# The turned keys of a chunked recurrence made by VectorE in 32x32 blocks, in four buffers, with the row norm in two halves

## What is computed

```python
def step(S, inp):                      # chunks of tokens
    L = jnp.cumsum(gc, axis=1)
    o_inter = jnp.einsum('bchk,bhkv->bchv', qc * jnp.exp(L), S)
    ...
    S_new = jnp.exp(Lc)[..., None] * S + jnp.einsum(
        'bjhk,bjhv->bhkv', kc * jnp.exp(Lc[:, None] - L), vc)
    return S_new, o_inter + o_intra
...
yb = rms_norm(o, o_norm_g).astype(x.dtype).reshape(B, T, WIDTH_B) * jax.nn.silu(zb)
```

## Time and profile before

| | before |
|---|---|
| median of 3 runs | 1557.94 us (1557.22 to 1558.79) |
| span of the profiled execution | 1555.9 us |
| PE busy | 1527.1 us, 98% |
| VectorE busy | 787.0 us, 51% |
| GpSimd busy | 826.0 us, 53% |
| ScalarE busy | 540.7 us, 35% |
| mean granted TensorE clock | 0.996 of full speed |

### The profile page before, as it was taken

One profiled execution on the slowest core, in us unless ns is written; L12 is line 12 of the kernel. 1 busy time (PEld: TensorE's weight loads), 2 busy tenths in 40 slices (PEclk: granted clock), 3 DMA queues, 4 the chain that ended last, 5 costly groups with the idle time before them and its releaser, 6 DMA issues.

```text
span 1555.9 us, 31655 instructions
## 1 busy us (share of the span) xinstructions
PE 1527.1 (98%) x13048; PEld 1243.0 (80%) x13048; DVE 787.0 (51%) x1900; ACT 540.7 (35%) x1119; POOL 826.0 (53%) x1074
## 2 busy tenths in 40 slices
PE   5999999999999999999999999999999999999998
PEld 2777788877888788888779878888888978888886
DVE  4767464234558866232544774622453775623132
ACT  4334324334322532434331452243432353143330
POOL 0525434557863643365773472437786363437671
PEclk9999999999999999999999999999999999999999
DMA  9612211334453321233343231223544231222351
GB/s 339 243 55 83 83 57 55 111 133 158 168 197 108 110 70 57 82 109 108 137 164 135 92 120 43 83 66 114 208 154 149 75 110 56 78 72 91 102 167 60
DMA packets 62790, 178.94 MB, mean 115 GB/s; under 512 B 7086, under 2 KB 18695, under 8 KB 61864
## 3 DMA queue, kind: packets, MB, share of 16 engines
q1 hardware_dynamic: 62648, 176.93, 33.4%
HBM read 162.84 MB, written 11.96 MB: 112 GB/s over the span
## 4 chain that ended last, share of the span: by engine, by line
PE 95%; DVE 3%; DMA 1%; SPq 1%; issue 1%; ACT 0%; DVEq 0%
PE ps_D L758 56%; PE ps_D L755 25%; PE ps_XCD L820 2%; PE ps_XB L896 1%; PE ps_XB L949 1%; PE ps_XA L954 1%; PE ps_XA L921 1%; PE ps_XA L932 1%; PE ps_XB L948 1%; PE ps_XA L896 1%; DMA th_t<-in_w_ada 1%; SPq L507 1%; PE ps_XB L932 0%; PE ps_XCD L831 0%; PE ps_XCD L939 0%
## 5 line engine op out<-in xcount | busy, mean ns | idle before, releaser
L1702 POOL TENSOR_TENSOR w_lo_t<-w_raw,w_hi_t 128x256 fp32r<-128x256 f32 x920 | 681.0, 775 | 599.7 <-ACT w_hi_t L980 599.4
L758 PE MATMUL ps_D<-h_hi_t,w_hi_t 128*128 128x512 f32 x1024 | 411.2, 402 | 0.0
L758 PE MATMUL ps_D<-h_hi_t,w_lo_t 128*128 128x512 f32 x1024 | 399.6, 390 | 0.0
L758 PE MATMUL ps_D<-h_lo_t,w_hi_t 128*128 128x512 f32 x1024 | 399.5, 390 | 0.0
L980 ACT ACTIVATE w_hi_t<-w_raw 128x1024 fp32r<-128x1024 f32 x232 | 240.0, 1051 | 124.6 <-PE ps_D L755 61.6
L758 PEld LDWEIGHTS ps_D<-h_hi_t,w_hi_t 128*128 128x128 f32 x1024 | 192.3, 188 | 46.3 <-issue 8.9
L758 PEld LDWEIGHTS ps_D<-h_hi_t,w_lo_t 128*128 128x128 f32 x1024 | 192.2, 188 | 41.8
L758 PEld LDWEIGHTS ps_D<-h_lo_t,w_hi_t 128*128 128x128 f32 x1024 | 192.6, 188 | 36.5
L755 PE MATMUL ps_D<-w_hi_t,h_hi_t 128*128 128x384 f32 (+1 forms) x384 | 141.6, 369 | 1.0 <-DVE yf_t L1342 1.0
L755 PE MATMUL ps_D<-w_lo_t,h_hi_t 128*128 128x384 f32 (+1 forms) x384 | 136.6, 356 | 0.0
L755 PE MATMUL ps_D<-w_hi_t,h_lo_t 128*128 128x384 f32 (+1 forms) x384 | 136.3, 355 | 0.0
(11 more groups left out here) (386 smaller groups left out, 2332.9 us busy)
## 6 DMA issues: line engine op xcount, KB each, us to landing
w_raw<-in_w_blocks SPq DMA_DIRECT2D x232, 512.0 KB, 3.4
xr<-in_x_prompt SPq DMA_DIRECT2D x16, 512.0 KB, 5.0
x_or_AT<-in_x_prompt SPq DMA_DIRECT2D x14, 512.0 KB, 4.8
out_dram<-xr SPq DMA_DIRECT2D x12, 512.0 KB, 2.8
x_or_AT<-in_x_turned SPq DMA_DIRECT2D x3, 1024.0 KB, 5.6
p_or_hf<-in_x_turned SPq DMA_DIRECT2D x3, 1024.0 KB, 6.2
out_dram<-xr SPq DMA_DIRECT2D x8, 256.0 KB, 2.0
ibtok<-vtok SPq DMA_DIRECT2D x8, 192.0 KB, 3.5
```

The source lines that it names most:

```text
L758: ins = mm(bank[:, :], w[:, s0, k0 + k, :], a[:, k, :], start=go, stop=end)
L1702: ins = g_.tensor_tensor(w_lo[:, c, k:k + 2], w_raw[:, n % NRAW, k:k + 2], f32(w_hi[:, c, k:k + 2]), ALU.subtract)
```

## The change

`KT` is VectorE's alone. `turn` transposes 16 blocks of 32 partitions by 4 heads by 32 columns from `kk` straight into `kst[:, t]`, then waits for them, and a memset of one column signals `kst`. PE's four transposes, ScalarE's copy and the use of XC are gone. `kst` has four buffers, one for each chunk, in memory that the silu of za (`silu_za`) has in the attention part and the residual rows later; what else used the old buffer is now `yst`. The KT tasks stand at halves 54, 55, 56 and 58, `o` stays at 57, 59, 61 and 63, `st` too but for chunk 0, which goes from 57 to 58. PE's `st` and ScalarE's part of `o` now wait for `kst`. `onorm` is two tasks of two chunks each, at halves 60 and 64.

```diff
--- before.py
+++ after.py
@@ -89,6 +89,7 @@
                                 ("q", 2): 3}.items()}
 OUT_AT = (56.5, 57.5, 58, 59.5, 60.5, 61, 61.5, 62.5)
 S_AT, PV_AT = (18, 20, 22, 25, 27, 30, 32, 35), (24, 29, 34, 38)
+KT_AT, ON_AT = (54, 55, 56, 58), (60, 64)
 TILED = S_AT + PV_AT + tuple(range(42, 56, 2))
 SPOT, HOLDER, ATTACH, BURST_AT, PAIR = [], [], {}, {}, {}
 COST = {"A": 3, "B": 3, "pa": 2, "pb": 2}
@@ -194,10 +195,11 @@
     for _l in range(7):
         at_half(it, 42 + 2 * _l, "level", _l, "XA" if _l % 2 else "XB")
     for _t in range(NT):
-        put(it, 28 + _t, 0, "KT", _t, "XC")
-        put(it, 28 + _t, 1, "o", _t, "XB")
-        put(it, 28 + _t, 1, "st", _t, "XA")
-    put(it, 32, 0, "onorm", 0)
+        at_half(it, KT_AT[_t], "KT", _t)
+        at_half(it, 57 + 2 * _t, "o", _t, "XB")
+        at_half(it, 57 + 2 * _t + (_t == 0), "st", _t, "XA")
+    for _r in range(2):
+        at_half(it, ON_AT[_r], "onorm", _r)
     for _t in range(NT):
         at_half(it, 67 + _t, "yT", _t, "XB" if _t % 2 else "XA")
     if it < NIT - 1:
@@ -389,17 +391,20 @@
...
+        first.close()
+        first = ExitStack()
+        kst = first.enter_context(nc.sbuf_tensor("k_turned", [P, NT, HB, P], F32))
         first.close()
...
@@ -933,10 +938,6 @@
                                          start=j == 0, stop=j == 4)
                             if (i, j) == (1, 4):
                                 s.done(ins, "XA_full")
-                elif task == "KT":
-                    s.wait_ge("lvl", 8 * it + 8)
-                    for h in range(HB):
-                        ins = tr(bank[:, P * h:P * h + P], kk[:, h, P * a:P * a + P], ident[:, :])
                 elif task == "o":
                     s.freed(it, "level", 6)
                     s.unit_left(it, "ib", a)
@@ -949,9 +950,9 @@
                         ins = mm(bank[:, P * h:P * h + P], AT[:, h, P * a:P * a + P], ibtok[:, a, P * h:P * h + P],
                                  start=not more, stop=True)
                 elif task == "st":
-                    s.freed(it, "KT", a)
+                    s.wait_ge("kst", NT * it + a + 1)
                     for h in range(HB):
-                        ins = mm(bank[:, P * h:P * h + P], kst[:, h, :], ibtok[:, a, P * h:P * h + P],
+                        ins = mm(bank[:, P * h:P * h + P], kst[:, a, h, :], ibtok[:, a, P * h:P * h + P],
                                  start=True, stop=True)
                 elif task == "yT":
                     s.wait_ge("on", 4 * it + a + 1)
@@ -1122,13 +1123,9 @@
                         s.wait_ge("smax", 2 * (8 * it + a) + m // 2 + 1)
                         fn(p_t[:, m, :], p_t[:, m, :], ACT.Exp, bias=negm[:, m:m + 1], accum_out=rsum[:, m:m + 1])
                     s.done(fn(esk, esk, ACT.Exp), "p_exp")
-                elif task == "KT":
-                    s.full(*key)
-                    if it or a:
-                        s.full(*((it, "st", a - 1) if a else (it - 1, "st", 3)))
-                    s.free(fn(kst[:, :, :], bank[:, :].rearrange("p (h n) -> p h n", h=HB), ACT.Copy), *key)
                 elif task == "o":
                     s.full(*key)
+                    s.wait_ge("kst", NT * it + a + 1)
                     if it or a:
                         s.freed(*((it, "o", a - 1) if a else (it - 1, "o", 3)))
                     fn(kk[:, :, P * a:P * a + P], bank[:, 0:512].rearrange("p (h n) -> p h n", h=HB), ACT.Copy)
@@ -1417,6 +1414,13 @@
                 r = a[:, :, 0:TB].rearrange("p h (n c r) -> p h n c r", c=2, r=w)
                 return r[:, :, :, 0, :], r[:, :, :, 1, :]
 
+            def turn(dst, t):
+
+                for i in range(0, P, 32):
+                    for j in range(0, P, 32):
+                        s.done(v.transpose(dst[j:j + 32, :, i:i + 32], kk[i:i + 32, :, P * t + j:P * t + j + 32]))
+                s.settle()
+
             def yf_slot(n):
                 s.wait_ge("yl", n - 1)
                 return yf[:, n % 2, :].rearrange("p (m n) -> p m n", m=4)
@@ -1545,11 +1549,15 @@
                         ins = stt(state[:, h, :], state[:, h, :], ff[:, h, P * a:P * a + 1], bank[:, P * h:P * h + P],
                                   ALU.mult, ALU.add)
                     free(ins, *key)
+                elif task == "KT":
+                    turn(kst[:, a], a)
+                    do(v.memset(idle[:, :], 0.0), "kst")
                 elif task == "onorm":
-                    s.freed(it, "o", 3)
-                    do(ts(oss, oss, 1.0 / P, EPS, ALU.mult, ALU.add))
-                    rsqrt(orst, oss, ow1, ow2)
-                    for t in range(NT):
+                    s.freed(it, "o", 2 * a + 1)
+                    c = slice(8 * a, 8 * a + 8)
+                    do(ts(oss[:, c], oss[:, c], 1.0 / P, EPS, ALU.mult, ALU.add))
+                    rsqrt(orst[:, c], oss[:, c], ow1[:, c], ow2[:, c])
+                    for t in (2 * a, 2 * a + 1):
                         o = kk[:, :, P * t:P * t + P]
                         s.done(tt(o, o, orst[:, HB * t:HB * t + HB].unsqueeze(2).broadcast_to([P, HB, P]), ALU.mult), "on")
                 elif task == "yT":
```

More of the change, by code:

```diff
@@ L380, in build @@
         acc = sb("acc_t", [P, TB])
-        kst = sb("kst_t", [P, HB, P])
+        yst = sb("yst_t", [P, HB, P])
         hS, yS = sb("hS_or_yS", [P, KT, 32]), sb("cT_or_ab", [P, KT, 32])
@@ L391, in build @@
         kTs = R2[:, 0:512].rearrange("p (b n) -> p b n", b=4)
-        ps_s = kst[0:8]
-        AT32 = kst[:, :, :].rearrange("p h (t i) -> p (h t) i", t=NT)
+        ps_s = yst[0:8]
+        AT32 = yst[:, :, :].rearrange("p h (t i) -> p (h t) i", t=NT)
         sq_in = ibS[:, 0:256]
@@ L396, in build @@
         qz_b = R3[:, :].rearrange("p (h b c) -> p h b c", h=HB, b=NS)
-        vrow, selbc = kst[0:NV, 0], kst[:, 1]
+        vrow, selbc = yst[0:NV, 0], yst[:, 1]
         first = ExitStack()
```

## The result

The changed kernel takes 1586.92 us, median of 4 runs (1585.88 to 1588.15), beside 1558.36 us (1557.22 to 1558.79) for the kernel before on the same chip: ratio 1.0187, 95% interval 1.0175 to 1.02, **28.6 us slower**. 1588.5 was predicted, with a range of 1577 to 1598. One run in experiment two had a mean granted clock of 0.845 and took 1713.75 us, so its time there is the median of the other three.

A forecast was written before the change was run, and what follows sets the result against it. PE, busy 98% of the span, was taken to bound the kernel. Losses of 14.7 us in blocks 1 to 3, 8.9 in block 0 and 6.8 for the clock make 30.4 over 1557.94: 1588.5 us, range 1577 to 1598.

The forecast's parts named there:

- The bound and the savings: PE's instruction list sets the time; work taken off it saves 7.9 us in all, 2.45 of it in block 0.
- 1.82 us saved each: Blocks 1 to 3: net PE time saved per block by removing the KT transposes, provided nothing waits.
- The step, 0.35 us with no overlap: VectorE's block transposes in a KT task start 0.35 us apart without overlapping, 5.6 us a task.
- Rival A: VectorE's block transposes overlap, step 0.20 us, task 3.4 us: about 4 us faster, 1554; chance 0.10.
- C: Rival: a shorter block, about 0.25 us a step, clock never lost: some 5 us slower, 1563; chance 0.08.
- The waits: PE waits for D1 0.9 us (2.8 in block 0) and at o 1 5.8 us (4.8 in block 0).
- o 3 needs that bank ... 3.7 us: Block 0: the half norm delays freeing XC, ScalarE waits for it, and PE waits 3.7 us at o 3.
- The clock, 1.7 us at four waits: TensorE's clock falls after each of the four o 1 waits, costing 1.7 us each, 6.8 in all.
- Rival B: No overlap of transposes, but the clock stays at 1.00: 23.6 us slower, 1581.5; chance 0.22.
- The stages: Recurrence stages grow: waits less savings give 4.9 us in each of blocks 1 to 3, 8.9 in block 0, before clock.
- The norm in halves: onorm split in two adds 15 small VectorE instructions, 3.6 us per block, costed at nothing outside block 0.
- Rival D: Block 0: ScalarE's late weight split makes GpSimd's half too late for unit 33; 1600 us and more; chance 0.05.

The follow-up runs named there:

- experiment two: The changed kernel with the two loops of a turn exchanged, so mostly the input's start partition changes instead of the output's: 1587.94 us, ratio 1.0189.
- experiment one: The changed kernel with each transposed block written into the partitions it is read from, so turned keys differ from the reference: 1558.77 us, ratio 1.0009.
- experiment six: The changed kernel with another table only: third turn behind the first state update, fourth behind the third, half norms at 62 and 64: 1558.0 us, ratio 1.0.
- experiment seven: The changed kernel with 24 unread identity products on PE ahead of o 1 in blocks 1 to 3, filling the wait: 1582.51 us, ratio 1.0157.
- experiment five: Two runs: the kernel before with only the norm in halves, 1557.56 us; the changed kernel with the norm whole at half 64, 1588.47 us.
- three: The changed kernel with a task's 16 block transposes replaced by one over 128 partitions and 512 columns, turned keys not the reference's: 1550.61 us, ratio 0.9954.
- four: The changed kernel with the first turn one half later, at 55, behind the evacuation that frees D1: 1587.27 us, ratio 1.0189.

## Why the prediction was right, point by point

- **The bound and the savings** held. "1.82 us saved each" was 1.97, block 0's 2.45 was 2.43, so 8.3 us in all for the 7.9 of the sum.
- **The step, 0.35 us with no overlap**, on which everything hung, was 0.334; a task was 5.46 us for my 5.6. The reading of the copies, 0.44 us apart because their start partitions change, was the right one of the two, and experiment one shows it is the partitions: 0.19 to 0.24 us a step where they stay, and 1558.8 us. The price of one block from the 640-element transpose, 0.32 us, was 0.303. Rival A is out, and C too, which would have needed 0.25.
- **The waits.** D1: 0.63 us for 0.9, and 2.53 for 2.8 in block 0. o 1: 5.54 for 5.8 (5.53 and 5.55 in blocks 2 and 3), and 4.32 for 4.8. All a little shorter, by the shorter turn. A stop costs some 0.26 us beyond its idle time (experiment six), which the sum did not have.
- **"o 3 needs that bank ... 3.7 us"** in block 0 was wrong in size: o 3 begins at 281.90, at most 0.3 us late. ScalarE did wait for XC, as the mechanism had it (timeline of ScalarE, block 0, beside the earlier trace rows):

```profile
277.94 0.88 ACT L1100 ACTIVATE smS<-smS,bm_half 128x8 f32<-128x8 f32 x4 [10.99 <-DVE smS L1405]
278.72 0.67 ACT L1048 ACTIVATE p_or_hf<-ps_D,bm_half 128x512 f32<-128x512 f32 x1
279.29 1.04 ACT L981 ACTIVATE w_hi_t<-w_raw 128x1024 fp32r<-128x1024 f32 x1
280.24 0.58 ACT L1131 ACTIVATE kk<-ps_XB 128x512 f32<-128x512 f32 x1
```

  The two sides of the difference were off, each counted from the start of the stage: o 2's evacuation was done 45.1 us into it and not 47.0, by four turns 0.15 us shorter each, a row task of the sample of 4.9 us for my 5.4 (its first multiply took 0.31 instead of the 0.80 of the earlier trace rows) and a half norm of 4.3 for my 4.9; and PE came 44.9 us into it and not 43.4, by the half clock behind o 1, which I had kept out of this chain. A small difference of two long chains took the errors of both.
- **The clock, 1.7 us at four waits**, was too low: 1.5, 2.6 and 2.5 by experiment seven in blocks 1 to 3. For block 0, half of its 3.4 us at 0.50 is 1.7, and what its stage of 6.8 us more leaves, with the saving of 2.43 and without the waits of 2.53, 4.32 and 0.3 and 0.5 for two stops, is 1.6. So about 8.3 us for the 6.8 of the sum. Rival B, no fall, is out: dense work ahead did not keep the clock. By the rule of the Trainium skill alone, as the prediction took it ("TensorE: Matmul & The Clock Gate", Part 1: The HAM clock gate), each fall would have cost the whole 2.5 and the sum been 3 us higher; the falls in blocks 2 and 3 did cost that.
- **The stages** are 6.3, 7.3 and 7.2 us longer in blocks 1 to 3, for 6.6 predicted (4.9 + 1.7), and 6.8 in block 0 for 10.6: 27.6 against 30.4.
- **Not foreseen** were the wait for issue in block 1 and the clock behind it, 4.4 us, which together with the shorter start (1.4 us, within what the start varies between these kernels) filled most of the gap. So the total is better than its parts, and that is luck: the o 3 term was some 3.4 us too high, the clock 1.5 too low, and 4.4 that nobody foresaw made up the rest. Without the o 3 term the forecast would have been 26.7, and 28.6 was measured.
- **The norm in halves, "at nothing"**, was shown twice (experiment five). **Rival D** didn't come: w_hi_t's split at 279.29 was in time.

## What to carry to other kernels

Before work moves to an engine that is half idle, find the task in its queue that the busy engine waits for, and add up what now stands ahead of it: here 91 us more on an engine with 49% to spare cost 29, because three turns of 5.4 us stood ahead of a state update of 1.1. When small instructions of VectorE step from one group of partitions to another, as these do, count each at its full length, since none of the 256 overlapped the next; then cut their number by putting more elements into each, which, with better places in the queue, turned this loss into a gain of 0.3%. And a wait on TensorE costs more than its idle time: here up to 2.6 us of half clock on top of 5.5.

## What was not expected of the hardware

- The clock fell behind every idle wait of 4.3 to 5.5 us. Behind shorter ones it fell in some kernels and not in others. Behind the wait of 1.64 us with only tiny products (128x32) ahead of it, it went to 0.69 and then 0.50, for some 3 us; behind the same wait of 1.50 to 1.65 us in experiments one, three and four it stayed at 1.00. Behind the D1 wait of 2.53 us in block 0 it fell with the norm whole (experiment five) and stayed at 1.00 in the changed kernel.
- The same wait and the same o 1 behind it cost 1.5 us in one block and 2.6 in another: full rate came back after 3.2 us of work in block 1 and only after 5.3 in block 2. Half rate ahead of another wait costs nothing (experiment five).
- TensorE can wait 0.3 to 1.7 us with no engine and no DMA of data as releaser, mostly in runs of tiny products but also among dense ones (0.99 and 1.48 us in experiment seven; the kernel before has one of 1.45 at 786.19). The places move when TensorE's instruction count ahead of them changes by 16. Differences of 2 to 3 us between kernels can be this alone, and 4.4 where the clock falls with it.
- VectorE's block transposes keep their time beside a GpSimd that is busy 52% of the span: 298 to 309 ns in all 256.
